# LayerNorm weight and bias moved from the rows into the copies of their transposes

## The chip, the cores and the metric

One core of a Trainium2 chip runs one program. The metric is the device time of one launch in microseconds (us), median over runs. The engines are TensorE (PE for its matmuls, PEld for its weight loads), VectorE (DVE), ScalarE (ACT), GpSimd (POOL) and SyncE (SP), which here only issues DMAs. Each has its own instruction stream; they meet only at semaphores.

## The reference

Two layers over 256 tokens of 1024 channels, all in float32. Each layer is a mixer and then a mixture of experts, and each of these four stages ends in a LayerNorm over the channels. Mixer 0 is an mLSTM beside an RG-LRU, mixer 1 an S5 state space model beside gated linear attention. The experts are 64, of which each token takes 8, plus a shared one. What matters here:

```
def layer_norm(x, w, b):
    xc = x - mean(x)
    y = xc * rsqrt(mean(xc * xc) + EPS)
    return y * w + b

for l in (0, 1):
    h = layer_norm(ALPHA * h + mixer_l(h) @ w_out[l], ln1_w[l], ln1_b[l])
    h = layer_norm(ALPHA * h + moe_l(h),              ln2_w[l], ln2_b[l])
```

ALPHA is the square root of 2. The output is the last h.

## The kernel before, in words

The stages mix0, moe0, mix1, moe1 follow one another on every engine; each engine walks through its own list of them. The 256 tokens are two tiles of 128 rows (t = 0 and 1, one token for each partition), held in `h` of 128 x 2 x 1024. Every stage first needs the transposed rows `hT`, 1024 channels in 8 chunks of 128 partitions by 256 tokens. PE transposes `h` chunk by chunk into four banks of PSUM (L653 in the mixers, L910 before the experts); ACT copies banks 0 and 2 to `hT`, DVE banks 1 and 3 (L1110 and L1326 in mixer 1, L1238 and L1751 before the experts). A copy takes one bank, two chunks, 128x512.

A stage ends in `dve_ln`. For each tile: the sum with the scaled residual (L1307, after the mixers only; after the experts PE has already added it in PSUM), statistics of both halves (L1310), their aggregation (L1312). Then DVE subtracts the mean and multiplies by the weight row `lnw`, half by half (L1316), while ACT takes the root of the variance (`act_ln`, L1281). DVE inverts it (L1320) and forms h, scaled by it, plus the bias row `lnb` (L1321). That signals `h_ready`. Weight and bias stand as rows, copied to every partition by DMA (`sp_ln_params`), and are overwritten for the next stage when `h_ready` says so.

`wait_h` makes the reader of a stage wait for `h_ready`. PE waits so before the transposes of each tile. In between it runs filler matmuls that compute nothing (`keep_clock`, L608): 8 before tile 0 in mixer 1, 5 before tile 1 in front of the experts. SP waits for the same signal before it loads the remaining first experts or the next mixer weights. In mixer 1 PE also runs 64 small matmuls (L640) between the tiles, whose result ACT copies in four parts (L1182) after its copies of the transposed rows. PE's next matmuls (L772) wait for all of these.

Before the experts PE computes router scores from `hT` (L925), and the shared expert's first product (L945) runs while DVE chooses the experts: L1684 adds the router's bias, a chain of small operations follows, and L1720 writes `chosen`. PE needs `chosen` at L951, in the middle of L945. Meanwhile ACT casts h to the upper part `h_top` (L1241, per tile) and GpSimd forms the rest `h_low` (L560, per tile). The router's sigmoid on ACT needs a table load before it. The expert loop then gathers rows from `h_top` and `h_low`, multiplies them with the experts' weights (L1040, L1070) and adds the results in PSUM (L971); its weights stream in by DMA.

The last stage's h goes out by DMA. At the start SP loads x, then a few parameters (L317), then the first mixer's weights (L265), which PE needs for L615.

## Time and profile before

| | |
|---|---|
| runs | 1323.25, 1323.59, 1326.84 us; median 1323.59 |
| profiled execution | 1326.38 us, span 1324.7 us, mean granted clock 0.985 |
| busy in the span | PE 1287.8 (97%), PEld 699.5, DVE 527.7 (40%), ACT 187.4 (14%), POOL 46.7 (4%) |
| chain that ended last | PE 92%, DVE 4%, DMA 3%, issue 1%, ACT 1% |
| the costliest lines of the chain | L1040 33%, L1070 17%, L971 10%, L992 9% |
| DMA | 462.33 MB, mean 349 GB/s |

The three inner boundaries lie near 152 us (mix0 to moe0), 661 us (moe0 to mix1) and 800 us (mix1 to moe1); the last norm begins near 1312 us.

How to read the rows below: a timeline row has the start, the busy time, the engine, the line of the kernel, the operation, what it writes and reads, how many instructions are merged into it, and in brackets how long the engine had been idle and what ended that. A float32 matmul or transpose is recorded as two instructions, so five filler matmuls are x10. A merged row's time runs from the first start to the last end. A table load (ACT_TABLE_LOAD) is ACT's change to the set of functions that its next operation needs.

### The profile page before, as it was taken

How to read it: one execution, taken by the hardware profiler on the slowest of the kernel's cores; microseconds unless marked ns; L12 is line 12 of the kernel's file. 1: busy time of each engine (PE TensorE's matmuls, PEld its weight loads, DVE VectorE, ACT ScalarE, POOL GpSimd, SP SyncE). 2: the span in 40 equal slices, each digit the busy share in tenths (PEclk: the TensorE clock that was granted, in tenths of full speed). 3: DMA queues.
4: the chain of work that ended last, by engine and by line, in shares of the span. 5: the costliest groups of instructions: out<-in, count | busy, mean ns of one | idle time of the engine just before them, and what ended most of it. 6: DMA issues, size and time to landing. Idle time of an engine off the chain costs nothing.

```text
span 1324.7 us, 16993 instructions
## 1 busy us (share of the span) xinstructions
PE 1287.8 (97%) x6753; PEld 699.5 (53%) x6753; DVE 527.7 (40%) x1071; ACT 187.4 (14%) x314; POOL 46.7 (4%) x76
## 2 busy tenths in 40 slices
PE   8979999999999999999999999999999999999996
PEld 6845564445544454445476656454445544454443
DVE  6777543333333333333336136233333333333324
ACT  3122201111111111111031212011111111111111
POOL 6200100000000000000010001000000000000000
PEclk9989999999999999999998998999999999999999
DMA  7853849999999999999952169499999999999992
GB/s 236 245 229 145 350 200 408 421 422 422 422 422 421 423 422 422 422 422 421 376 184 83 33 252 421 166 402 420 421 422 423 422 422 422 422 423 422 421 421 113
DMA packets 77625, 462.33 MB, mean 349 GB/s; under 512 B 9680, under 2 KB 10896, under 8 KB 27152
## 3 DMA queue, kind: packets, MB, share of 16 engines
q1 hardware_dynamic: 77584, 461.74, 86.0%
q8 instruction: 30, 0.49, 0.1%
q14 instruction: 11, 0.09, 0.0%
HBM read 455.36 MB, written 6.36 MB: 349 GB/s over the span
## 4 chain that ended last, share of the span: by engine, by line
PE 92%; DVE 4%; DMA 3%; issue 1%; ACT 1%; SPq 0%; DVEq 0%; ACTq 0%
PE bank L1040 33%; PE bank L1070 17%; PE bank L971 10%; PE bank L992 9%; PE bank L615 4%; PE bank L625 4%; PE bank L945 2%; PE bank L673 2%; PE bank L687 2%; PE bank L1051 1%; DMA expert_weights<-s_rows 1%; PE bank L1004 1%; DVE expert_weights L1531 1%; PE bank L980 1%; DMA weight_ring<-in_w_in_even 1%; PE bank L795 1%
## 5 line engine op out<-in xcount | busy, mean ns | idle before, releaser
L1070 PE MATMUL bank<-expert_weights,hiddenT 128*64 128x512 f32 x1024 | 233.8, 598 | 2.0 <-DVE hiddenT L1807 2.0
L1040 PE MATMUL bank<-expert_weights,hT 128*64 128x512 f32 x1024 | 225.3, 592 | 0.0
L1040 PE MATMUL bank<-expert_weights,weight_ring 128*64 128x512 f32 x1024 | 225.2, 592 | 0.0
L1804 DVE TENSOR_TENSOR hidden<-silu_gate,bank 128x256 f32<-128x256 f32 x64 | 26.9, 421 | 330.0 <-ACT silu_gate L1262 330.0
L1040 PEld LDWEIGHTS bank<-expert_weights,weight_ring 128*64 128x64 f32 x1024 | 74.5, 137 | 145.2 <-issue 145.2
L1040 PEld LDWEIGHTS bank<-expert_weights,hT 128*64 128x64 f32 x1024 | 73.4, 137 | 145.3 <-issue 145.0
L1070 PEld LDWEIGHTS bank<-expert_weights,hiddenT 128*64 128x64 f32 x1024 | 68.2, 136 | 119.7 <-issue 110.7
L992 PE MATMUL bank<-onehot_r,h_top 128*128 128x256 f32 x512 | 125.5, 288 | 0.0
L992 PE MATMUL bank<-onehot_r,h_low 128*128 128x256 f32 x512 | 119.7, 277 | 0.0
L971 PE MATMUL bank<-y_top,onehotT_r 128*128 128x512 f32 x264 | 111.8, 423 | 0.0
L971 PE MATMUL bank<-y_low,onehotT_r 128*128 128x512 f32 x264 | 104.5, 396 | 0.0
L992 PEld LDWEIGHTS bank<-onehot_r,h_low 128*128 128x128 f32 x512 | 96.4, 188 | 0.0
L992 PEld LDWEIGHTS bank<-onehot_r,h_top 128*128 128x128 f32 x512 | 96.3, 188 | 0.0
L615 PE MATMUL bank<-hT,weight_ring 128*128 128x256 f32 x384 | 86.5, 388 | 0.4 <-DMA weight_ring<-in_w_in_even 0.4
L971 PEld LDWEIGHTS bank<-y_top,onehotT_r 128*128 128x128 f32 x264 | 49.4, 187 | 61.8 <-issue 52.4
L1262 ACT ACTIVATE silu_gate<-bank 128x256 f32<-128x256 f32 x64 | 24.5, 383 | 397.9 <-PE bank L1040 397.9
L1266 ACT ACTIVATE y_top<-bank,slot_gate 128x512 fp32r<-128x512 f32 x64 | 44.0, 687 | 259.5 <-PE bank L1070 259.5
L615 PEld LDWEIGHTS bank<-hT,weight_ring 128*128 128x128 f32 x384 | 74.4, 195 | 11.9 <-DMA weight_ring<-in_w_in_even 0.9
L1814 DVE TENSOR_SCALAR y_top<-bank,slot_gate 128x512 fp32r<-128x512 f32 x64 | 48.0, 751 | 78.4 <-PE bank L1070 78.4
L1821 DVE SCALAR_TENSOR_TENSOR y_low<-bank,slot_gate,y_top 128x512 fp32r<-128x512 f32 x64 | 48.0, 751 | 57.5 <-ACT y_top L1266 57.5
L625 PE MATMUL bank<-weight_ring,hT 128*128 128x512 f32 x128 | 58.3, 612 | 8.6 <-DVE gate_cols L1385 8.6
L1807 DVE COPY hiddenT<-bank 128x256 f32<-128x256 f32 x64 | 27.1, 424 | 92.3 <-PE bank L1051 92.3
(359 smaller groups left out, 1073.6 us busy)
## 6 DMA issues: line engine op xcount, KB each, us to landing
expert_weights<-in_exp_w_gate SPq DMA_DIRECT2D x128, 1024.0 KB, 11.1
expert_weights<-in_exp_w_up SPq DMA_DIRECT2D x128, 1024.0 KB, 13.9
expert_weights<-in_exp_w_down SPq DMA_DIRECT2D x128, 1024.0 KB, 13.2
weight_ring<-in_w_in_even SPq DMA_DIRECT2D x6, 2048.0 KB, 10.3
weight_ring<-in_w_out SPq DMA_DIRECT2D x4, 2048.0 KB, 7.4
weight_ring<-in_w_in_odd SPq DMA_DIRECT2D x4, 2048.0 KB, 10.1
s_c<-expert_weights SPq DMA_DIRECT2D x1, 3072.0 KB, 8.7
expert_weights<-s_c SPq DMA_DIRECT2D x1, 3072.0 KB, 10.9
```

The lines of the kernel that those rows point to most:

```text
L615: last = nc.tensor.matmul(B.tile(f"{name}{i}")[:, a * SEQ:(a + 1) * SEQ], w[:, c, (2 * i + a) * P:(2 * i + a + 1) * P], hT[:, c, :], start ...
L625: last = nc.tensor.matmul(B.tile(f"{name}{t}")[:, :], hT[:, c, t * P:(t + 1) * P], w[:, c, :], start=(c == 0), stop=(c == KC - 1))
L673: last = nc.tensor.matmul(bank[2 * t + n][:, :], mixT[:, m0 + m, t * P:(t + 1) * P], w[:, m, n * 512:(n + 1) * 512], start=(m == 0), stop= ...
L971: last = nc.tensor.matmul(bank[2 * t + n][:, :], onehotT[:, par, t, :], part[:, n * 512:(n + 1) * 512], start=False, stop=(done and part i ...
L992: last = nc.tensor.matmul(bank[banks[k // 2]][:, (k % 2) * SEQ:(k % 2 + 1) * SEQ], part[:, t, c, :], onehot[:, t, :, :].rearrange("p a s - ...
L1040: last_mm = nc.tensor.matmul(bank[6][a * CAP:(a + 1) * CAP, :].rearrange("p (w f) -> p w f", w=2), xq[:, c, s0:s0 + CAP], ew_gu(2 * u + a, c),
L1070: last_mm = nc.tensor.matmul(bank[b][a * CAP:(a + 1) * CAP, :], hm[:, j, a * CAP:(a + 1) * CAP], ew_d(2 * u + a)[:, j, half * 512:(half + ...
L1266: nc.scalar.activation(y_top[:, 512:1024], bank[5][:, :], ACT.Copy, scale=slot_gate[:, u:u + 1])\
L1804: nc.vector.tensor_tensor(hslot[:, :], sg[:, :], bank[6][:, DE:2 * DE], ALU.mult)\
L1807: nc.vector.tensor_copy(hm[:, :, :], bank[7][:, 0:JE * P].rearrange("p (j s) -> p j s", j=JE))\
L1814: nc.vector.tensor_scalar(y_top[:, 0:512], bank[4][:, :], slot_gate[:, u:u + 1], None, ALU.mult)\
L1821: nc.vector.scalar_tensor_tensor(out=y_low[:, 512:1024], in0=bank[5][:, :], scalar=slot_gate[:, u:u + 1], in1=y_top[:, 512:1024], op0=ALU. ...
```

## The change

Weight and bias are no longer applied to the rows that get transposed. After the norm of the first three stages DVE forms only x_hat, mean taken off and multiplied by the inverse deviation, in `resid`, and signals `x_hat`. PE transposes x_hat, and `wait_h` waits for that signal, as SP does. In the transposed rows a channel is a partition, so weight and bias are columns (`lncols`, a new 128x48 load at the start), and the copies to `hT` apply them: ACT with `Identity`, scale and bias, DVE with a multiply and an add, each chunk of 128x256 by itself, so two instructions where one copy was. The rows of h are made later (`dve_h`, two operations of 128x1024 for each tile): before the experts, tile 0 inside the norm and tile 1 behind the turned copies; in mixer 1 both behind the copies. ACT's cast to `h_top` now waits for `h_ready`. The last norm (`dve_ln_out`) keeps the product with the weight row, but behind root and reciprocal. `act_ln` starts with a root of a constant, one column, so that the table is asked for before the statistics arrive. Filler goes from 8 matmuls to 2 in mixer 1 and from 5 to 3 before the experts. `wts` now shares the buffer of `masked`, and the mixers share two semaphores.

```diff
         def pe_transposes(pe, B, st):
             for t in range(TT):
                 if stage_no[st] and t == 0:
-                    keep_clock(pe, 7, 8)
+                    keep_clock(pe, 7, 2)
...
-                                                   h[:, t, :].rearrange("p (q c) -> p c q", c=KC)[:, c, :],
-                                                   ident[:, :])
+                                                   (resid if stage_no[st] else h)[:, t, :]
+                                                   .rearrange("p (q c) -> p c q", c=KC)[:, c, :], ident[:, :])
...
                 if t:
-                    keep_clock(pe, 0, 5)
+                    keep_clock(pe, 0, 3)
...
         def act_moe(act, l, chain):
...
-                nc.scalar.copy(hT[:, 2 * b:2 * b + 2, :], bank[4 + b][:, :].rearrange("p (c t) -> p c t", c=2))\
-                  .then_inc(m["hT_a"], 1)
-            for t in range(TT):
+                for c in range(2):
+                    last = act_turned_rows(2 * l, 2 * b + c, bank[4 + b][:, c * SEQ:(c + 1) * SEQ])
+                last.then_inc(m["hT_a"], 1)
+            for t in range(TT):
+                act.wait_ge(S["h_ready"], TT * 2 * l + t + 1)
                 nc.scalar.copy(h_top[:, t, :, :], ...).then_inc(m["top_parts"], 1)
...
         def act_ln(act, k):
             act.wait_ge(S["consts"], N_CONSTS)
+            nc.scalar.activation(spare1[:, 0:1], epsc[:, 0:1], ACT.Sqrt)
...
+        def act_turned_rows(k, c, src):
+            return nc.scalar.activation(hT[:, c, :], src, ACT.Identity, bias=lncols[:, k, 1, c:c + 1],
+                                        scale=lncols[:, k, 0, c:c + 1])
...
+        def dve_ln_stats(dve, chain, k, t, src, summed):
+            for n in range(2):
+                dve.wait_ge(summed, 2 * t + n + 1)
+                if k % 2 == 0:
+                    chain.link(nc.vector.scalar_tensor_tensor(out=src[n], in0=h[:, t, n * 512:(n + 1) * 512],
+                                                              scalar=ALPHA, in1=bank[2 * t + n][:, :],
+                                                              op0=ALU.mult, op1=ALU.add))
+                last = nc.vector.bn_stats(stats[:, t, n, :], src[n])
+            chain.link(last)
+            nc.vector.bn_aggr(mv[:, t, :], stats[:, t, :, :]).then_inc(S["ln_stats"], 1)
+            dve.wait_ge(S["ln_std"], TT * k + t + 1)
+            chain.link(nc.vector.reciprocal(rstd[:, t:t + 1], rstd[:, t:t + 1]))
+
         def dve_ln(dve, chain, k, summed):
             for t in range(TT):
                 src = [bank[2 * t + n][:, :] if k % 2 else resid[:, t, n * 512:(n + 1) * 512] for n in range(2)]
+                dve_ln_stats(dve, chain, k, t, src, summed)
                 for n in range(2):
+                    last = nc.vector.tensor_scalar(resid[:, t, n * 512:(n + 1) * 512], src[n], mv[:, t, 0:1],
+                                                   rstd[:, t:t + 1], ALU.subtract, ALU.mult)
+                last.then_inc(S["x_hat"], 1)
+                if k % 2 == 0 and t == 0:
+                    dve_h(dve, chain, k, t)
+
+        def dve_h(dve, chain, k, t):
+            dve.wait_ge(S["x_hat"], TT * k + t + 1)
+            dve.wait_ge(LN[k]["params"], 32)
+            chain.link(nc.vector.tensor_tensor(h[:, t, :], resid[:, t, :], lnw[:, :], ALU.mult))
+            nc.vector.tensor_tensor(h[:, t, :], h[:, t, :], lnb[:, :], ALU.add).then_inc(S["h_ready"], 1)
+
+        def dve_ln_out(dve, chain, k, summed):
+            for t in range(TT):
+                src = [bank[2 * t + n][:, :] for n in range(2)]
+                dve_ln_stats(dve, chain, k, t, src, summed)
+                dve.wait_ge(LN[k]["params"], 32)
+                for n in range(2):
+                    last = nc.vector.scalar_tensor_tensor(out=resid[:, t, n * 512:(n + 1) * 512], in0=src[n],
+                                                          scalar=mv[:, t, 0:1], in1=lnw[:, n * 512:(n + 1) * 512],
+                                                          op0=ALU.subtract, op1=ALU.mult)
                 chain.link(last)
...
                 nc.vector.scalar_tensor_tensor(out=h[:, t, :], in0=resid[:, t, :], scalar=rstd[:, t:t + 1],
                                                in1=lnb[:, :], op0=ALU.mult, op1=ALU.add).then_inc(S["h_ready"], 1)
+
+        def dve_turned_rows(k, c, src):
+            return nc.vector.tensor_scalar(hT[:, c, :], src, lncols[:, k, 0, c:c + 1], lncols[:, k, 1, c:c + 1],
+                                           ALU.mult, ALU.add)
...
         def dve_mix1(dve, chain):
-            wait_h(dve, "mix1")
             for row in (1, 3):
-                dve_copies(dve, B, f"T{row}", hT[:, 2 * row:2 * row + 2, :])
+                dve.wait_ge(*B.full(f"T{row}"))
+                for c in range(2):
+                    last = dve_turned_rows(1, 2 * row + c, B.tile(f"T{row}")[:, c * SEQ:(c + 1) * SEQ])
+                last.then_inc(B.done["d"], 1)
+            for t in range(TT):
+                dve_h(dve, chain, 1, t)
...
         def dve_moe(dve, l, chain):
...
-                nc.vector.tensor_copy(hT[:, 2 * b:2 * b + 2, :], bank[4 + b][:, :].rearrange("p (c t) -> p c t", c=2))\
-                  .then_inc(m["hT_d"], 1)
+                for c in range(2):
+                    last = dve_turned_rows(2 * l, 2 * b + c, bank[4 + b][:, c * SEQ:(c + 1) * SEQ])
+                last.then_inc(m["hT_d"], 1)
+            dve_h(dve, chain, 2 * l, 1)
             dve.wait_ge(m["halves"], 1)
```

## Rows read from the trace of the kernel before

**Rows 1.** Timeline, first boundary: start us, us, engine line op out<-in, [idle <-releaser].

```profile
152.22 0.69 DVE L1307 SCALAR_TENSOR_TENSOR resid<-h,bank 128x512 f32<-128x512 f32 x1 [1.04 <-PE bank L687]
...
152.90 2.32 PE L608 MATMUL bank<-hT,ident 128*128 128x256 f32 x10
...
153.68 0.21 DVE L1312 BATCH_NORM_AGGREGATE ln_mean_var<-ln_stats 128x2 f32<-128x12 f32 x1
...
153.92 0.29 ACT L1281 ACTIVATE ln_rstd<-ln_mean_var,eps 128x1 f32<-128x1 f32 x1 [6.51 <-DVE ln_mean_var L1312]
...
156.79 1.16 PE L910 MATMUL bank<-ident,h 128*128 128x128 f32 x8 [1.56 <-DVE h L1321]
...
157.54 1.29 DVE L1751 COPY hT<-bank 128x512 f32<-128x512 f32 x2 [0.81 <-PE bank L910]
...
158.27 4.07 ACT L1241 CAST h_top<-h 128x1024 fp32r<-128x1024 f32 x2
...
160.43 5.68 POOL L560 TENSOR_TENSOR h_low<-h,h_top 128x1024 fp32r<-128x1024 f32 x2 [120.03 <-ACT h_top L1241]
...
171.01 0.29 DVE L1720 TENSOR_TENSOR chosen<-replaced,masked 128x128 f32<-128x128 f32 x1
...
171.73 0.33 PE L951 MATMUL bank<-chosen,upper_strict 128*128 128x64 f32 x2
```

**Rows 2.** Timeline of the second boundary, moe0 to mix1.

```profile
663.14 1.28 ACT L1281 ACT_TABLE_LOAD   x1 [3.31 <-DVE ln_mean_var L1312]
...
664.43 3.62 PE L608 MATMUL bank<-hT,ident 128*128 128x256 f32 x16
...
664.44 0.29 ACT L1281 ACTIVATE ln_rstd<-ln_mean_var,eps 128x1 f32<-128x1 f32 x1
...
666.17 1.29 DVE L1310 BATCH_NORM_STATS2 ln_stats<-bank 128x6 f32<-128x512 f32 x2
...
667.49 0.21 DVE L1312 BATCH_NORM_AGGREGATE ln_mean_var<-ln_stats 128x2 f32<-128x12 f32 x1
...
668.87 1.53 PE L640 MATMUL bank<-expert_weights,gathered_xT 128*32 128x96 f32 x64
...
670.59 1.16 PE L653 MATMUL bank<-ident,h 128*128 128x128 f32 x8 [0.19 <-DVE h L1321]
...
672.07 1.91 ACT L1182 COPY expert_weights<-bank 32x384 f32<-32x384 f32 x4
...
674.19 1.07 PE L772 MATMUL bank<-hT,w_gates 128*32 128x256 f32 x16 [2.45 <-ACT expert_weights L1182]
```

**Rows 3.** Windows, first boundary then third: busy us (count) by engine, clock, DMA.

```profile
158.93:162.81 3.88, 3.88 (x26) 3.08 (x27) 1.61 (x3) 3.86 (x3) 2.38 (x1) 1.00 1.00 414
...
807.07:813.86 6.79, 6.79 (x26) 4.54 (x27) 2.52 (x4) 4.67 (x3) 5.24 (x2) 0.55 1.02 425
```

**Rows 4.** Groups by form: count, busy us, mean ns, idle before.

```profile
L1531 DVE TENSOR_TENSOR expert_weights<-expert_weights 128x1024 f32<-128x1024 f32 x6 | 7.2, 1222 | 8.5 <-DMA expert_weights<-s_rows 8.4
...
L1568 DVE TENSOR_SCALAR expert_weights<-bank,cols_odd 128x256 f32<-128x256 f32 x2 | 0.9, 479 | 16.8 <-PE bank L781 16.8
...
L1550 DVE TENSOR_SCALAR expert_weights<-expert_weights 128x512 f32<-128x512 f32 x1 | 0.4, 426 | 0.0
...
L1222 ACT ACTIVATE expert_weights<-bank,cols_odd 128x256 f32<-128x256 f32 x4 | 1.7, 470 | 4.2 <-PE bank L868 4.2
```

**Rows 5.** Chain of waits at the end: start us, us, engine line.

```profile
1318.55 0.22 DVE ln_mean_var L1312
...
1318.80 1.41 DVE resid L1316 x2
```

**Rows 6.** Line L1684: count, ns min/median/max, first and last start us.

```profile
L1684 DVE TENSOR_TENSOR biased<-scores,router_bias x2: 292/1295/2298, 164.0 to 814.6; 128x128 f32<-128x128 f32 x2
```

**Rows 7.** Timeline of the start.

```profile
2.89 0.65 SPq L317 DMA_DIRECT2D cols_even<-in_cols_even  x1
...
16.88 14.08 PE L615 MATMUL bank<-hT,weight_ring 128*128 128x256 f32 x64 [0.41 <-DMA weight_ring<-in_w_in_even]
```

More of the change, by code:

```diff
@@ L383, in sp_moe @@
             if k:
-                sp.wait_ge(S["h_ready"], TT * k)
+                sp.wait_ge(S["x_hat"], TT * k)
             for s in range(early, NSLOT):
@@ L1175, in act_mix1 @@
             B = B1
-            act_copies(act, B, "T0", hT[:, 0:2, :])
-            act_copies(act, B, "T2", hT[:, 4:6, :])
+            for row in (0, 2):
+                act.wait_ge(*B.full(f"T{row}"))
+                for c in range(2):
+                    last = act_turned_rows(1, 2 * row + c, B.tile(f"T{row}")[:, c * SEQ:(c + 1) * SEQ])
+                last.then_inc(B.done["a"], 1)
             act.wait_ge(M1["direct"], 1)
@@ L1299, in dve_ln @@
         def dve_ln(dve, chain, k, summed):
-            ln = LN[k]
             for t in range(TT):
                 src = [bank[2 * t + n][:, :] if k % 2 else resid[:, t, n * 512:(n + 1) * 512] for n in range(2)]
+                dve_ln_stats(dve, chain, k, t, src, summed)
                 for n in range(2):
-                    dve.wait_ge(summed, 2 * t + n + 1)
-                    if k % 2 == 0:
-                        chain.link(nc.vector.scalar_tensor_tensor(out=src[n], in0=h[:, t, n * 512:(n + 1) * 512],
-                                                                  scalar=ALPHA, in1=bank[2 * t + n][:, :],
-                                                                  op0=ALU.mult, op1=ALU.add))
-                    last = nc.vector.bn_stats(stats[:, t, n, :], src[n])
-                chain.link(last)
-                nc.vector.bn_aggr(mv[:, t, :], stats[:, t, :, :]).then_inc(S["ln_stats"], 1)
-                dve.wait_ge(S["ln_stats"], TT * k + t + 1)
-                dve.wait_ge(ln["params"], 32)
-                for n in range(2):
-                    nc.vector.scalar_tensor_tensor(out=resid[:, t, n * 512:(n + 1) * 512], in0=src[n],
-                                                   scalar=mv[:, t, 0:1], in1=lnw[:, n * 512:(n + 1) * 512],
-                                                   op0=ALU.subtract, op1=ALU.mult)
-                dve.wait_ge(S["ln_std"], TT * k + t + 1)
-                chain.link(nc.vector.reciprocal(rstd[:, t:t + 1], rstd[:, t:t + 1]))
@@ L1663, in dve_head_norm @@
                 last = nc.vector.tensor_tensor(hmv[:, :, :, 1], hmv[:, :, :, 1], hrs[:, :, :], ALU.add)
-            last.then_inc(M["hstat"], 1)
-            dve.wait_ge(M["hstd"], 1)
+            last.then_inc(M0["hstat"], 1)
+            dve.wait_ge(M0["hstd"], 1 if center else 2)
             chain.link(nc.vector.reciprocal(hrs[:, :, :], hrs[:, :, :]))
@@ L1857, in _ @@
                     dve_moe(dve, int(st[-1]), chain)
-                dve_ln(dve, chain, stage_no[st], {"mix0": M0["out_full"], "mix1": M1["out_full"],
+                (dve_ln if stage_no[st] < len(stages) - 1 else dve_ln_out)(dve, chain, stage_no[st], {"mix0": M0["out_full"], "mix1": M1["out_full"],
                                                   "moe0": MO[0]["acc_full"], "moe1": MO[1]["acc_full"]}[st])
@@ L1904, in packed, with by_chunk @@
     bt = b.reshape(P, 2, 4, 4, 32).transpose(2, 4, 1, 3, 0)
-    return {"cols_even": even, "cols_odd": odd, "b_odd": b.reshape(P, -1), "c_odd": c.reshape(P, -1),
+    def by_chunk(name, l):
+        return np.asarray(inputs[name])[l].reshape(P, KC)
+    ln = np.stack([np.stack([by_chunk(f"ln{n}_{w}", l) for w in "wb"], axis=1) for n, l in ((1, 0), (2, 0), (1, 1))], axis=1)
+    return {"ln_cols": np.ascontiguousarray(ln.reshape(P, -1), dtype=np.float32), "cols_even": even, "cols_odd": odd, "b_odd": b.reshape(P, -1), "c_odd": c.reshape(P, -1),
             "bt_odd": bt.reshape(P, -1)}
```

26 lines of the change are left out of this document (15 added, 11 removed).

## The prediction

> **What bounds the kernel now.** I read the page first, its busy shares and its chain of waits: PE is busy for 97% of the span and makes up 92% of the chain. Then the list of what PE waited for, to find the few places where it stands still: they add up to under 30 us, and about 10 us of them lie at the three inner boundaries between stages, where a layer norm on DVE and ACT is all that PE can wait for. Last the timeline of each boundary. In the first (mixer 0 to experts 0) PE ends its projection at 152.20; DVE works off the last half tile, and PE transposes the second tile only at 156.79, though the filler matmuls L608 ran out at 155.22 [rows 1]. It stands still again until the copies of the turned rows (L1238, L1751) are done, and goes on at 158.93. The second boundary has the same shape, with a table load on ACT that starts only when the statistics are there, and PE goes on at 674.19 [rows 2]. The third repeats the first to a few hundredths of a microsecond up to L925. After each boundary PE runs without a gap that matters, so what is won or lost there reaches the end; DMA is late nowhere in the expert loops.
>
> The third boundary shows one thing more. From 807.07 to 813.86 the granted clock averages 0.55, nearly all of it at half, the lower level (1.2 GHz). The same 26 records, L925 and the first eight of L945, take 6.79 us there and 3.88 us at the first boundary [rows 3]: a fall of the clock costs 2.91 us. PE had stood still 1.55 us, worked 1.16, stood still 0.98. The first boundary, with the same gaps, kept the clock.
>
> **The base of the sum.** The profiled execution took 1326.38 us (span 1324.7 and 1.7 around it). The runs are 1323.25, 1323.59 and 1326.84. Profile less 2.91 is 1323.47, so I read the median as an execution without a fall, and two of the four executions as having had one.
>
> **The change, part by part.** Tile 0 and tile 1 are the two halves of 128 tokens.
>
> *First boundary, the norm.* After the aggregation DVE now waits for ACT's root (0.03 to start, 0.29, 0.02), does the reciprocal (about 0.2 with its wait), then two subtract-and-multiply of 128x512 from SBUF. Such an instruction with one column takes 0.43 us [rows 4]; the pair of two-tensor ones that it replaces takes 1.41 [rows 5]. Two columns can't be under one: the pair lies between 0.85 and 1.41, I take 1.0. From the aggregation's end (153.89) to the transposes this makes 0.35 + 0.2 + 1.0 + 0.04 = 1.6 where 2.90 stood. But tile 0 now also makes its h inside the norm: root and reciprocal 0.55, the pair 1.0, two tensor operations of 128x1024 at 1.22 [rows 4] with their wait 2.5, together 4.05 against 2.8 (the 2.90 above, less the start of PE). DVE had 1.04 us of room before tile 1's last half [rows 1]; it comes 1.2 later, so 0.2 late. Gain 1.1 (0.7 to 1.4): transposes at 155.7.
>
> *The turned copies.* Two copies of 128x512 on DVE (1.29) become four of 128x256 with two columns. With one column two take 0.88, so about 0.40 apart [rows 4]; four are 1.7 to 1.95, I take 1.8: 0.5 more (0.35 to 0.7). ACT's four at 470 ns each, some 0.37 apart [rows 4], end before them. PE starts L925 0.6 earlier than before.
>
> *Routing.* The h of tile 1 (2.45 us) now stands behind the copies on DVE, 158.3 to 160.8. ACT's cast of tile 1 waits for it: 160.8 to 162.8, then the table load 1.28 and the scores at 164.4, against 163.9. GpSimd's h_low moves too, 5.68 us of work from about 160.8 to 166.5. The row that matters is L1684: 128x128, 2.30 us at the first boundary (from 164.0), ending 0.2 after h_low [rows 1]; at the third, with h_low over before, the same takes 0.29 [rows 6]. So DVE stood behind GpSimd for 2 us. After the change it is released at about 166.6, 0.35 later than now, and with it L1720. Chosen was ready at 171.30 and PE asked at 171.73 [rows 1]; PE comes 0.6 earlier and chosen 0.35 later, so PE waits about 0.35. Net gain 0.25 at this boundary (-0.4 to 0.6), and the same at the third.
>
> *Second boundary.* The root's table is asked for ahead, in an idle stretch of ACT, so 1.28 us leave tile 0. Tile 0: from the aggregation 0.35 + 0.2, then a pair that reads PSUM, where I take 1.45 (1.41 is the pair of the same width now); x_hat at 665.1, where h came when L1310 of tile 1 could start, about 666.2 [rows 2]. Tile 1's statistics follow at once, 1.3 and 0.25 with the aggregation; then 0.55 + 1.45: transposes at 668.6, not 670.59 [rows 2], 2.0 earlier. Filler is 2 matmuls, not 8 (3.62 us, [rows 2]), and ends about when x_hat comes. ACT then reaches L1182 1.48 after the transposes start now (672.07 less 670.59 [rows 2]) and 0.5 later with four copies for two, about 2.0; the 1.91 of L1182, which PE waits for, follow as now. PE goes on at 672.7 to 672.8, gain 1.4 (0.9 to 1.9). The four tensor operations of h (4.9 us) lie under L615, with 14 us to spare before DVE's next reader. SP's loads wait for x_hat and start earlier; its LN parameters wait for h, with nothing urgent behind them.
>
> *The end.* The last norm keeps its form, but the two products now stand behind root and reciprocal, 0.35 + 0.2, where 1.41 of them ran beside the root and only 0.08 of reciprocal showed [rows 5]. For tile 1 that costs 0.5. In tile 0 the saved table load pays for it. Loss 0.55.
>
> *The start.* One more load stands before the first weights on SP; its like (cols_even) took 0.65 us to issue [rows 7]. PE waits for these weights, 0.41 us at 16.88 [rows 7], and the chain of mixer 0 hangs on it. The DMA engines are already full there, so between 0 and 0.65, I take 0.5. Everything else (semaphores, the shared buffer for weights, one more tiny root in the mixer norms, under ACT's idle time) costs nothing.
>
> Sum at full clock: +0.5 - 0.25 - 1.4 - 0.25 + 0.55 = -0.85, so 1322.6.
>
> *The clock.* PE's idle time grows although its work starts sooner. At the second boundary it now stands still 2.44 us [rows 2]; afterwards about 0.65 (from 667.9, when the filler, tile 0's transposes and the 1.53 of L640 are through [rows 2], to 668.6), 1.16 of transposes, then 3.1. At the first and third: 1.35 and 1.55 instead of 1.56 and 0.98, with three filler matmuls for five. The clock fell once in half of the executions with shorter gaps than these. I therefore expect one fall in the typical execution, most likely at the second boundary, at the 2.91 us of [rows 3].
>
> At the second boundary the table load starts at 663.14, when the statistics are there, takes 1.28, and the root starts at 664.44 [rows 2]: nothing but the load stands in between. The Trainium skill, "ScalarE: Activation LUTs" (What ACT_TABLE_LOAD costs), gives about 1283 ns for the load and about 1380 ns more for a drain, 2.66 us for a switch. The trace agrees with the load and shows no room for the drain; by the page's switch the gain of that boundary would be some 1.4 larger, an estimate, and the sum 1321.2 at full clock. The row decides.
>
> **The rivals.**
> - *No fall of the clock:* 1322.6. For it: in two of four executions there was none, and the second boundary kept it with 2.44 us of rest.
> - *Two falls or more:* 1322.6 + 5.8 = 1328.4, slower. All three boundaries have longer gaps than before. Against: in no execution shown does the time ask for two.
> - *DVE loses its turn to GpSimd* (the other side): if ACT's cast of tile 0 ends before the second operation of tile 1's h has started, h_low goes first. By my times the cast ends at 159.9 and that operation starts at 159.6, only 0.3 us apart. The operation then waits until 162.85, h comes at 164.1, the cast 166.15, h_low ends at 169.05, L1684 at 169.3, chosen at 174.35, PE having asked at 171.1 to 171.3. That is 2.7 more at two boundaries: 1322.6 + 5.4 = 1328.0. It decides from 0.3 us of delay on DVE. That one of the two shuts the other out is what L1684 shows, 2.30 beside h_low and 0.29 without [rows 6]. The Trainium skill, "SBUF — State Buffer" (Who interferes with whom), has it as a rule: a Vector instruction with two SBUF inputs and a GpSimd one that reads SBUF exclude each other for the whole instruction, whichever starts first; by that rule, the trace agrees.
> - *The table load doesn't move,* or stays behind the wait: 1.3 is lost at the second boundary and 1.3 at the end against the sum, so 1325.2 without a fall.
>
> **How the numbers follow.** One fall 0.45: 1322.6 + 2.9 = 1325.5, its own range 1323.8 to 1327.3 from the bounds above. No fall 0.26. Two falls 0.12, lost turn 0.08, table load 0.04, something not seen 0.05. A difference of 0.3% is 4.0 us, about what can be told from no change. Slower needs 1327.6: most of two falls and lost turn, 0.16. Faster needs 1319.6, beyond the best ends of all terms (about 1321): 0.04. Same 0.80. Range 1321.5 to 1328.5.
>
> **What would show it.** Right: no table load behind the statistics at the second boundary and the end; transposes 1.1 and 2.0 us after a shorter wait than now; L1720 some 0.35 later against the projection's end, with a short wait of PE at L951; half clock in a window behind the second boundary. Wrong: a first operation of h on DVE of 1.2 and a second of over 3 us (the lost turn); full clock behind all three boundaries (then 1322.6); the weights at the start later by more than 0.65.

## The result, and the profile after

| | before | after |
|---|---|---|
| median of the runs beside each other | 1325.19 us (7 runs, 1323.12 to 1326.84) | 1330.94 us (7 runs, 1327.24 to 1332.37) |
| ratio after / before | | 1.0042, 95% interval 1.0027 to 1.0058 |
| profiled execution, its span | 1326.38, 1324.7 us | 1330.94, 1328.5 us |

The change makes the kernel slower by 0.4%. The forecast was 1325.5 with a range up to 1328.5: the time lies outside, on a side that had been given 0.16.

The span grew by 3.8 us. To find where, I took the same few instructions in both traces as marks and subtracted:

| stretch, from mark to mark | before | after | difference |
|---|---|---|---|
| start to tile 0's transposes before experts 0 | 152.02 | 153.59 | +1.57 |
| to the shared expert's down product (L1004, now L1007) | 25.40 | 26.47 | +1.07 |
| experts 0, to the first statistics of their norm | 484.10 | 486.30 | **+2.20** |
| second boundary, to mixer 1's first product (L772, now L775) | 12.67 | 11.67 | -1.00 |
| mixer 1, to tile 0's transposes before experts 1 | 125.98 | 126.24 | +0.26 |
| third boundary, to L1004, now L1007 | 28.31 | 25.25 | -3.06 |
| experts 1, to the first statistics of the last norm | 484.11 | 486.33 | **+2.22** |
| the last norm, to the end | 12.07 | 12.62 | +0.55 |
| sum | | | +3.81 |

The -3.06 at the third boundary is mostly the clock: the profile before had its fall there (2.91 us, [rows 3]), while the profile after has one at the first boundary and one at the second.

The two bold rows are the surprise. The change touches nothing inside the expert loops, no wait in them grew, and both are longer by the same 2.2 us. The groups of instructions by form show one line that is slower, the gather; the line below is one of its neighbours, which is not. First the kernel before (columns as in [rows 4]):

```profile
L992 PE MATMUL bank<-onehot_r,h_top 128*128 128x256 f32 x512 | 125.5, 288 | 0.0
L992 PE MATMUL bank<-onehot_r,h_low 128*128 128x256 f32 x512 | 119.7, 277 | 0.0
L971 PE MATMUL bank<-y_low,onehotT_r 128*128 128x512 f32 x264 | 104.5, 396 | 0.0
```

After:

```profile
L995 PE MATMUL bank<-onehot_r,h_top 128*128 128x256 f32 x512 | 129.5, 291 | 0.0
L995 PE MATMUL bank<-onehot_r,h_low 128*128 128x256 f32 x512 | 124.1, 281 | 0.0
L974 PE MATMUL bank<-y_low,onehotT_r 128*128 128x512 f32 x264 | 104.5, 396 | 0.0
```

A loop has 512 of these matmuls, half with each part, so 2.2 us are 4.3 ns for each. The view of one line in a narrow window shows that it is every matmul and not a few late ones: minimum, median and maximum in ns, of eight with h_top, in the middle of the loop, before:

```profile
L992 PE MATMUL bank<-onehot_r,h_top x8: 276/276/369, 404.8 to 406.5; 128*128 128x256 f32 x8
```

and after:

```profile
L995 PE MATMUL bank<-onehot_r,h_top x8: 277/281/367, 408.5 to 410.2; 128*128 128x256 f32 x8
```

The boundaries did about what was forecast. The first, to be read against [rows 1]:

```profile
155.58 0.29 ACT L1290 ACTIVATE ln_rstd<-ln_mean_var,eps 128x1 f32<-128x1 f32 x1 [6.67 <-DVE ln_mean_var L1323]
155.91 0.16 DVE L1325 RECIPROCAL ln_rstd<-ln_rstd 128x1 f32<-128x1 f32 x1 [0.36 <-ACT ln_rstd L1290]
156.11 1.00 DVE L1333 TENSOR_SCALAR resid<-resid,ln_mean_var,ln_rstd 128x512 f32<-128x512 f32 x2
...
157.16 1.16 PE L913 MATMUL bank<-ident,resid 128*128 128x128 f32 x8 [1.23 <-DVE resid L1333]
...
157.69 1.93 ACT L1295 ACTIVATE hT<-bank,ln_cols 128x256 f32<-128x256 f32 x4 [1.81 <-PE bank L913]
157.92 1.90 DVE L1362 TENSOR_SCALAR hT<-bank,ln_cols 128x256 f32<-128x256 f32 x4 [0.81 <-PE bank L913]
...
159.92 3.60 PE L928 MATMUL bank<-hT,router_w 128*64 128x256 f32 x16 [1.60 <-ACT hT L1295]
160.98 1.23 DVE L1344 TENSOR_TENSOR h<-h,ln_b 128x1024 f32<-128x1024 f32 x1
161.67 6.09 POOL L563 TENSOR_TENSOR h_low<-h,h_top 128x1024 fp32r<-128x1024 f32 x2 [121.44 <-ACT h_top L1249]
...
166.32 1.59 DVE L1729 TENSOR_TENSOR biased<-scores,router_bias 128x128 f32<-128x128 f32 x1
```

The transposes come 3.57 after those of tile 0 (157.16 less 153.59; 4.77 before), the pair L1333 takes the 1.0 that was forecast, and L928 takes 3.60 where it took 1.95: the clock fell, the granted clock averages 0.52 from 159.92 to 163.45. The second boundary, against [rows 2]:

```profile
664.70 1.28 ACT L1287 ACT_TABLE_LOAD   x1
...
665.99 0.20 ACT L1287 ACTIVATE table_load<-eps 128x1 f32<-128x1 f32 x1
...
666.36 1.29 DVE L1321 BATCH_NORM_STATS2 ln_stats<-bank 128x6 f32<-128x512 f32 x2 [0.76 <-PE bank L974]
...
672.00 1.53 DVE L1333 TENSOR_SCALAR resid<-bank,ln_mean_var,ln_rstd 128x512 f32<-128x512 f32 x2
...
673.58 1.16 PE L656 MATMUL bank<-ident,resid 128*128 128x128 f32 x8 [0.92 <-DVE resid L1333]
674.11 1.93 ACT L1295 ACTIVATE hT<-bank,ln_cols 128x256 f32<-128x256 f32 x4 [2.34 <-PE bank L656]
...
675.92 1.90 ACT L1188 COPY expert_weights<-bank 32x384 f32<-32x384 f32 x4
...
678.03 1.16 PE L775 MATMUL bank<-hT,w_gates 128*32 128x256 f32 x16 [3.29 <-ACT expert_weights L1188]
```

The table load is over before the statistics start. And the end, the chain of waits (start, us, what), against [rows 5]: root and reciprocal now stand in front of the products.

```profile
1322.16 0.30 ACT ln_rstd L1290
1322.47 0.02 issue
1322.49 0.17 DVE ln_rstd L1325
1322.67 0.03 issue
1322.69 1.42 DVE resid L1353 x2
```

### The profile page after: what moved, and what is told of

It is laid out like the page before. It is cut to its first block, busy times and chain, and to the rows that moved or that the text cites. A ratio compares the mean times of both kernels' runs of the same rounds, so it can differ in the third digit from the quotient of the medians.

```text
span 1328.5 us, 16971 instructions
## 1 busy us (share of the span) xinstructions
PE 1284.2 (97%) x6733; PEld 697.1 (52%) x6733; DVE 536.8 (40%) x1083; ACT 191.1 (14%) x324; POOL 47.3 (4%) x76
## 4 chain that ended last, share of the span: by engine, by line
PE 90%; DVE 5%; DMA 3%; ACT 1%; issue 1%; SPq 0%; DVEq 0%
PE bank L1043 33%; PE bank L1073 17%; PE bank L974 10%; PE bank L995 9%; PE bank L618 4%; PE bank L628 4%; PE bank L676 2%; PE bank L948 1%; PE bank L1054 1%; DMA expert_weights<-s_rows 1%; PE bank L1007 1%; DVE expert_weights L1572 1%; PE bank L690 1%; PE bank L983 1%; DMA weight_ring<-in_w_in_even 1%
## 5 line engine op out<-in xcount | busy, mean ns | idle before, releaser
L995 PE MATMUL bank<-onehot_r,h_top 128*128 128x256 f32 x512 | 129.5, 291 | 0.0
L995 PE MATMUL bank<-onehot_r,h_low 128*128 128x256 f32 x512 | 124.1, 281 | 0.0
```

The lines of the kernel that those rows point to most:

```text
L995: last = nc.tensor.matmul(bank[banks[k // 2]][:, (k % 2) * SEQ:(k % 2 + 1) * SEQ], part[:, t, c, :], onehot[:, t, :, :].rearrange("p a s - ...
```

## The experiments

**What could lengthen one matmul of the loop?** The change put two new buffers in front of others in SBUF: `ln_cols` (192 bytes per partition) and `table_load` (32 with its rounding). Everything allocated behind them moved. `onehot`, which the gather streams, went from byte 183360 to 183584, that is from 64 to 32 beyond a multiple of 128. Moving the buffers behind all others tests it:

```diff
-        lncols = sb("ln_cols", [P, 3, 2, KC])
...
-        spare1 = sb("table_load", [P, 1])
...
         prm = sb("s5_work", [P, 13, NT])
+        lncols = sb("ln_cols", [P, 3, 2, KC])
+        spare1 = sb("table_load", [P, 1])
```

> The changed kernel with ln_cols and table_load allocated behind all other buffers, so that onehot starts at byte 183360 of a partition again instead of 183584; no instruction differs. Theory A (the gather matmuls L995 are slower because onehot, their moving operand, now starts at 32 beyond a multiple of 64 bytes): 16 of them take 1.83 us again instead of 1.90, each expert loop 473.0 and 484.1 us on the same stretches instead of 475.2 and 486.3, the kernel about 4.4 us faster than the changed one (near 1326.5). Theory B (something in the changed instruction streams, or in what h and h_top hold, slows the loops): the loops stay 2.2 us longer each and the time stays near 1330.9.

Measured: 1325.28 us (12 runs), ratio to the kernel before 0.9993 (0.9979 to 1.0007); expert stages of 483.97 us each.

```profile
L995 PE MATMUL bank<-onehot_r,h_top 128*128 128x256 f32 x512 | 125.2, 287 | 0.0
L995 PE MATMUL bank<-onehot_r,h_low 128*128 128x256 f32 x512 | 119.4, 277 | 0.0
```

So the slowdown of the loops is where the buffers lie, and without it the changed kernel can't be told from the kernel before. Then the same the other way round, the kernel before with 32 unused bytes and no other edit:

```diff
+        pad = sb("pad", [P, 8])
         onehot_at = next_offset()
```

> The kernel before with 32 unused bytes in front of onehot, which then starts at 183392, 32 beyond a multiple of 64; nothing else differs. Theory A: the gather matmuls L992 take 1.90 us for 16, each expert loop 2.2 us longer, the kernel about 4.4 us slower than before (near 1329.6 against 1325.2). Theory B: no difference from before.

Measured: 1329.57 us (10 runs), ratio 1.0038 (1.0023 to 1.0053), expert stages of 486.05 us. Its groups:

```profile
L993 PE MATMUL bank<-onehot_r,h_top 128*128 128x256 f32 x512 | 129.0, 291 | 0.0
L993 PE MATMUL bank<-onehot_r,h_low 128*128 128x256 f32 x512 | 123.5, 280 | 0.0
```

This is 4.36 us above the kernel before (1325.21), as theory A had it. Every buffer behind onehot moves with it in these kernels; that onehot is the one that counts rests on the gather being the only one of the costly groups that loses more than 2 ns (L971 with y_top goes from 423 to 425).

**Which starts are good?** The same edit in the changed kernel (onehot at 64 beyond a multiple of 128), and one of 64 bytes in the kernel before (at 0).

> The changed kernel with 32 more unused bytes in front of onehot: it starts at 183616, a multiple of 64 that neither kernel had. Theory A: gather back at 1.83 us for 16, loops 4.4 us shorter together. If instead the old address itself or the distance to another buffer mattered, it stays at 1.90. Theory B: stays at 1.90.

> The kernel before with 64 unused bytes in front of onehot: start 183424, a multiple of 64 and of 128 (before it was 64 beyond a multiple of 128). Theory A with 64 bytes as the unit: gather at 1.83 us for 16 as before. If a coarser or another boundary counts: another value, shorter or longer than 1.83.

Measured: the first 1325.13 us (one run), expert stages 484.3 and 484.2, 287 and 277 ns: fast. The second 1328.32 us (one run), 486.57 for each, 292 and 281 ns: slow, so a multiple of 64 is not enough. Next I moved everything from the weight ring on by 64, the gather's two stationary parts with it (h_top lies in `resid`, h_low in the ring):

```diff
+        pad = sb("pad", [P, 16])
         wring_at = next_offset()
```

> The kernel before with 64 unused bytes per partition in front of the weight ring, so that the ring (with h_top and h_low in it), h, hT, resid and onehot all start 64 bytes further: onehot at 0 beyond a multiple of 128 as in the slow kernel with 64 bytes in front of onehot alone, but as far from h_top and h_low as in the kernel before. Theory 1, the distance between onehot and h_top/h_low decides: the gather matmuls stay at 288 and 277 ns, 16 of them at 1.83 us, the expert loops at 473.0 and 484.1 us, time about 1325. Theory 2, onehot's own start decides (fast only 64 beyond a multiple of 128): 292 and 281 ns, 1.90 us, loops at 475.3 and 486.3, time about 1329.

Measured: 1324.87 us, 484.0 and 484.1, 287 and 277 ns, with onehot at the same start modulo 128 as in the slow kernel ahead of it. So not onehot's own start decides, but how it stands to other buffers. Which? First h_top and onehot together, h_low left (the same line, in front of `resid_at`):

> The kernel before with 64 unused bytes in front of resid, so that h_top (which lies in resid) and onehot start 64 bytes further and h_low (in the weight ring) stays: the distance from h_top to onehot is again 64 beyond a multiple of 128, that from h_low to onehot is 0. Theory 1a, the distance between onehot and the rows that the same matmul holds decides: the h_top group stays at 287 to 288 ns, the h_low group goes to 280 to 281, each loop 1.1 us longer, time 1327. Theory 1b, the distance between onehot as it streams and the rows that are being loaded for the next matmul decides (half of each part's loads lie under the other part): both groups in between, 290 and 279. Rival, the start of h_top or h_low alone decides: one of 1a's numbers would come with no change in the other kernel whose every start was moved, which stayed at 288 and 277, so then both stay or both change.

Measured: 1329.05 us, 486.3 for each, and both groups slow, where theory 1a had wanted h_top's to stay fast and 1b half of each:

```profile
L993 PE MATMUL bank<-onehot_r,h_top 128*128 128x256 f32 x512 | 129.0, 292 | 0.0
L993 PE MATMUL bank<-onehot_r,h_low 128*128 128x256 f32 x512 | 123.7, 281 | 0.0
```

Neither form held. Three more separate the two parts from each other and from their neighbours: h_top alone moved (64 bytes in front of `resid`, 64 in front of onehot), h_low alone (below), and h_low with onehot (below, with `ln_stats` behind onehot and 32 bytes in its place).

```diff
-        wring = sb("weight_ring", [P, 2, KC * 512])
+        wring = sb("weight_ring", [P, 2, KC * 512 + 16])
...
-            offset=wring_at + 4 * (KC * 512 * (ring_no[f"sh_d{l}"] % 2) + JE * D))
+            offset=wring_at + 4 * ((KC * 512 + 16) * (ring_no[f"sh_d{l}"] % 2) + JE * D) + 64 * (1 - ring_no[f"sh_d{l}"] % 2))
```

> The kernel before with h_top's start 64 bytes further (resid moved), h_low where it was, and onehot 128 bytes further, so still 64 beyond a multiple of 128. Starts modulo 128: h_top 64, h_low 0, hT 0, onehot 64. Theory L, the distance from h_low to onehot must be 64: fast, 287 and 277 ns, expert stages of 484.0 us. Theory B, the distances from both parts must be 64: slow, 292 and 281 ns, 486.3 us. Theory N, it is counted from something else that lies with the weight ring, h or hT: fast, as L.

> The kernel before with 64 unused bytes behind each of the two slots of the weight ring and h_low at 64 beyond a multiple of 128 in its slot; h, hT, h_top and onehot move by 128. Starts modulo 128: h_top 0, h_low 64, hT 0, onehot 64. Theory L: slow, 281 and 292 ns, expert stages of 486.3 us. Theory B: slow too. Theory N: fast, 484.0 us.

> The same with onehot 64 bytes nearer, at a multiple of 128. Starts modulo 128: h_top 0, h_low 64, hT 0, onehot 0. Theory L: fast, 287 and 277 ns, expert stages of 484.0 us, although onehot lies where it was slow. Theory B: slow, 486.3 us. Theory N: slow, 486.3 us.

Measured: 1328.04, 1327.77 and 1330.78 us (one run each). All kernels in one table, starts modulo 128:

| h_top | h_low | onehot | expert stages, us | kernels |
|---|---|---|---|---|
| 0 | 0 | 64 | 484.0 to 484.3 | before; changed with the buffers moved; changed with 32 bytes |
| 64 | 64 | 0 | 484.0 to 484.1 | before, all moved by 64 |
| 0 | 0 | 32 | 486.3 | the change |
| 0 | 0 | 96 | 486.1 | before with 32 bytes |
| 0 | 0 | 0 | 486.6 | before with 64 bytes |
| 64 | 0 | 0 | 486.3 | h_top and onehot moved |
| 64 | 0 | 64 | 485.7 | h_top alone |
| 0 | 64 | 64 | 486.3 | h_low alone |
| 0 | 64 | 0 | 485.5 | h_low and onehot |

Theories L and N fall with the last three rows. What is left is theory B: as fast as before only where onehot starts 64 beyond a multiple of 128 from both parts. Theory B alone doesn't give the sizes, and they differ: where the distance to h_top alone is right (rows six and eight) the cost is all of the 2.3 us, where that to h_low alone is (rows seven and nine) it is 1.5 to 1.7. Nor does it give which group is slow: with h_top alone moved (row seven) h_top's takes 289 ns and h_low's stays at 277, where theory B had 292 and 281; with h_low and onehot moved (row nine) they take 290 and 282. Most rows rest on one profile, but its two expert stages agree within 0.15 us in each. Why 64, and which access meets which, stays open.

**The table load alone.** The kernel before with the early root in `act_ln` and nothing else of the change:

```diff
             act.wait_ge(S["consts"], N_CONSTS)
+            nc.scalar.activation(spare1[:, 0:1], epsc[:, 0:1], ACT.Sqrt)
```

> The kernel before with one thing of the change: ACT asks for the root's table ahead of each norm, by a root of one column of a constant (its output column behind all other buffers, onehot stays). The products that ran beside the load (1.41 us) cover it and the root except for some 0.25 us. Theory: the table load is gone from the second boundary and the end, and each gains 0.25 us: 1324.7. Rival: the load is placed in front of the real root all the same, and nothing changes.

Measured: 1323.72 us (10 runs), ratio 0.9998 (0.9985 to 1.0010): not to be told from no change in the time, but plain in the trace. The end takes 11.71 us where 12.07 stood, the second boundary 12.41 where 12.67 stood. There the load is over 0.38 before the statistics, and root and first product start together:

```profile
660.91 1.28 ACT L1280 ACT_TABLE_LOAD   x1
...
662.20 0.20 ACT L1280 ACTIVATE table_load<-eps 128x1 f32<-128x1 f32 x1
662.57 1.29 DVE L1312 BATCH_NORM_STATS2 ln_stats<-bank 128x6 f32<-128x512 f32 x2 [0.77 <-PE bank L972]
...
664.15 0.29 ACT L1283 ACTIVATE ln_rstd<-ln_mean_var,eps 128x1 f32<-128x1 f32 x1 [1.74 <-DVE ln_mean_var L1314]
664.15 1.41 DVE L1318 SCALAR_TENSOR_TENSOR resid<-bank,ln_mean_var,ln_w 128x512 f32<-128x512 f32 x2
```

**Start and end undone.** From here on the changed kernel has its buffers at the end. The `ln_cols` load goes behind the first two blocks of weights, and `dve_ln_out` gets its old order back, the reciprocal behind the products:

```diff
-                dve_ln_stats(dve, chain, k, t, src, summed)
+                for n in range(2):
+                    dve.wait_ge(summed, 2 * t + n + 1)
+                    last = nc.vector.bn_stats(stats[:, t, n, :], src[n])
+                chain.link(last)
+                nc.vector.bn_aggr(mv[:, t, :], stats[:, t, :, :]).then_inc(S["ln_stats"], 1)
+                dve.wait_ge(S["ln_stats"], TT * k + t + 1)
                 dve.wait_ge(LN[k]["params"], 32)
...
+                dve.wait_ge(S["ln_std"], TT * k + t + 1)
+                chain.link(nc.vector.reciprocal(rstd[:, t:t + 1], rstd[:, t:t + 1]))
```

> The changed kernel with its two new buffers behind all others (so onehot starts where it did before), the ln_cols load behind the first two blocks of weights, and the last norm in the old order (products beside the root). Theory: both losses that were not in the expert loops are undone, 0.8 to 1.0 us at the start and 0.55 at the end less 0.26 for the table load now asked for early; against the version with only the buffers moved (1325.3) it is 1.3 to 1.8 faster: 1323.7, faster than the kernel before by about 1.1 us (0.1%), which five rounds may just tell. Rival: the start is no dearer by that load (the first filler-free matmul of mixer 0 came at 16.4 to 17.1 us in kernels with and without it), then 1324.7 and no difference from before.

Measured: 1323.92 us (12 runs), ratio 0.9987 (0.9971 to 1.0003). The end takes 11.72 us, 0.90 less than after the change. The start can't be told: the first matmul on the weights came at 16.87 us here; it comes at 16.42 to 17.90 in the four profiles with the load in front, and at 16.03 to 17.14 in the other thirteen.

**The filler.** The counts back to 8 and 5:

```diff
-                    keep_clock(pe, 7, 2)
+                    keep_clock(pe, 7, 8)
...
-                    keep_clock(pe, 0, 3)
+                    keep_clock(pe, 0, 5)
```

> The changed kernel with the two new buffers moved to the end and the filler back at 8 and 5 matmuls. At the old counts the filler ends 4.9 us after the statistics of tile 0 at the second boundary and delays tile 1's transposes by less than 0.1 us; before the experts it ends 0.4 us ahead of x_hat. Theory 1, the shortened filler is what lets the clock fall: full clock behind all three boundaries in the profile, a mean 2 to 3 us under that of the version with 2 and 3 (1324.8), so about 1322.3. Theory 2, the falls come with the shape of the boundaries (two short waits with a burst of transposes between) whatever the filler: one or two falls as before, time 1325 within 0.7.

Measured: 1326.52 us (12 runs), ratio 1.0014 (0.9997 to 1.0032). In its one profile theory 1 is half right: behind the second boundary the clock stayed (L775 1.07, its successors 14.08), behind the first it fell all the same. The time forecast from it, 1322.3, did not come. And my price for the filler was wrong: eight matmuls end after x_hat and put the transposes 8.81 after the first statistics (672.09 less 663.28), where two leave them at 7.22. So 1.6 us are paid at each launch for a fall saved, which in mixer 1 costs 0.6 to 2.3 (below).

**Work in the waits instead.** A filler ahead of the transposes delays them. The idle time behind them is longer (3.29 and 1.60), and nothing can be delayed there as long as the filler is shorter than the wait. A new helper multiplies the identity by itself, since `hT` is being written then. The filler ahead of the transposes goes from 2 to 3 and from 3 to 5 in the same edit, so against the last version two things change:

```diff
+        def keep_short(pe, b, count):
+            for _ in range(count):
+                nc.tensor.matmul(bank[b][:, 0:P], ident[:, :], ident[:, :], start=True, stop=True)
...
-                    keep_clock(pe, 7, 2)
+                    keep_clock(pe, 7, 3)
...
+            if stage_no[st]:
+                keep_short(pe, 3, 20)
             for b in range(4):
                 pe.wait_ge(*B.read(f"T{b}"))
...
-                    keep_clock(pe, 0, 3)
+                    keep_clock(pe, 0, 5)
...
+            keep_short(pe, 0, 9)
             pe.wait_ge(m["hT_a"], 2)
```

> The changed kernel as in the last version (buffers moved, ln_cols later, last norm in the old order), with PE kept busy in the waits that followed each burst of transposes: 20 matmuls of 128x128 on the identity (about 145 ns each, 2.9 us) in the 3.29 us ahead of mixer 1's first product, 9 (1.3 us) in the 1.60 us ahead of the router's product, and the filler ahead of tile 1 at 5 and at 3. None of it is longer than the wait that it fills. Theory: half clock behind the second boundary (in every profile with the filler at 2) and behind one of the other two comes from PE standing still there, so it goes: full clock behind all three, about 2.0 us less in mixer 1 and 1.5 to 2.9 at the first or third, 1323.9 less 3.5 to 4.9, 1319.0 to 1320.4: faster than the kernel before by 0.3%. Rival: the clock falls whatever PE does there, 1323.9 with half clock in the same places.

> The kernel before with the same short matmuls in its own waits behind the transposes: 15 (2.2 us) in the 2.45 us ahead of mixer 1's first product, 6 (0.9 us) in the 0.98 us ahead of the router's. Theory: as most profiles of this form show one fall at one of the three boundaries, 1.5 to 2.9 us go: 1324.8 less 2.2, 1322.6, and full clock behind all three. Rival: the wait of 1.55 us ahead of tile 1's transposes, which stays, is what lets the clock fall, then 1324.8 with a fall at the first or third boundary.

Measured: 1323.99 us (12 runs), ratio 0.9992 (0.9981 to 1.0002), and for the kernel before with 15 and 6 of them 1325.55 us (12 runs), 1.0007 (0.9996 to 1.0018). In both profiles the clock stayed full behind all three boundaries, as the theory said. That is not the filler ahead of the transposes alone: with 8 and 5 there and the waits empty the clock fell at the first boundary, and the kernel before had the same 8 and 5. But the time did not come. One part is that 40 records of L616 took 4.63 us, 231 ns for each matmul and not 145, so the filling outlasted the waits. In mixer 1 that costs 1.1 us (the second boundary takes 12.78 for 11.67). Before the experts L936 starts 0.35 late, and it costs nothing: the stretch to the shared expert's down product stays at 25.25, because PE would have waited for `chosen`. The falls saved are 3.25 us against the profile of the last version (26.23 less 25.25 at the first boundary, 127.67 less 125.40 in mixer 1), so 2.1 should have been left. In the profile mixer 0, where nothing was changed, took 2.2 us longer (154.00 for 151.76) and offset them; whether it does so in the median too no run shows. In the kernel before, 15 and 6 outlast the waits as well (13.50 for 12.67 at the second boundary, 25.68 for 25.39 at the others), but mixer 1 is 2.2 shorter (123.79 for 125.97), so its median of 1325.55 stays unexplained. (The 145 ns were a transpose's, eight in 1.16 us. A transpose is one record here, as x8 for eight chunks in [rows 1] shows, and not two as said above; a float32 matmul is two, 28 records for 14.) Cut to 14 and 6:

> The last changed version with its filling cut to the waits: a short matmul takes 231 ns where it was taken for 145, so 20 of them outlasted mixer 1's wait by 1.1 us and 9 the router's by 0.35. Now 14 (3.2 us in 3.29) and 6 (1.45 in 1.60). Theory: full clock behind all three boundaries as with 20 and 9, and the 1.8 us of overrun are back: 1324.0 less 1.8, 1322.2, faster than the kernel before by 0.1 to 0.2%. Rival: without the overrun the clock falls again behind the second boundary, then the overrun's 1.1 us are traded for a fall and the time stays at 1324. In the profiles mixer 0 varies by 3.5 us (its end at 150.5 to 154.0 us) with half clock at 60 to 90 us, so only the mean over runs can tell 2 us, and barely.

Measured: **1320.51 us** (6 runs, 1317.36 to 1321.89), ratio 0.9967 (0.9954 to 0.9980), the one version that beats both kernels. Its timeline, first and second boundary:

```profile
155.15 1.16 PE L920 MATMUL bank<-ident,resid 128*128 128x128 f32 x8 [0.37 <-DVE resid L1341]
156.15 1.50 PE L616 MATMUL bank<-ident 128*128 128x128 f32 x12
157.91 1.95 PE L936 MATMUL bank<-hT,router_w 128*64 128x256 f32 x16 [0.26 <-ACT hT L1303]
...
669.00 3.29 PE L616 MATMUL bank<-ident 128*128 128x128 f32 x28
672.45 1.07 PE L782 MATMUL bank<-hT,w_gates 128*32 128x256 f32 x16 [0.16 <-ACT expert_weights L1196]
```

L936 at 1.95 and L782 at 1.07 are the durations at full clock, against 3.60 and up to 1.93 at half. The waits left, 0.26 and 0.16, show that the filling now fits. From the first statistics to L782 it takes 11.67 us (672.45 less 660.78), as after the change, so nothing is paid for it. Against the profile of the version with empty waits it saves 1.0 at the first boundary and 2.1 in mixer 1, together 3.1, and the medians differ by 3.4 (1323.92 less 1320.51): this the trace explains. Against 20 and 9 matmuls the medians differ by 3.5, and the fit is worth only 1.1 of it (11.67 for 12.78); 2.4 lie in mixer 0 in the two profiles (151.57 for 154.00), and six runs don't settle how much of that is chance.

## Why the prediction was wrong

**The step that failed** is the sentence at the end of the start: "Everything else (semaphores, the shared buffer for weights, ...) costs nothing". The two new buffers are not even in that list. They cost 2.20 and 2.22 us in the expert loops, 4.4 of the 5.4 us between forecast and result. With that undone and all else as changed, the time is 1325.28, and the forecast had been 1325.5. That agreement is luck: two errors cancel, the base and the clock. The forecast was 1.9 us above the median that it started from (1323.59), and measured beside the kernel before, the version with the buffers moved is 0.07 above it, with an interval that ends at 0.9.

- *The base.* I read 1323.59 as an execution without a fall. It was the median of three; the later medians are 1325.19 (7 runs), 1325.21 (23), 1324.45 (29), 1324.49 (23) and 1324.37 (11). The three profiles of this form with a fast gather and empty waits (before, all moved by 64, table alone) have one fall each. So the usual execution seems to hold a fall already, and the base was 0.8 to 1.6 too low.
- *First and third boundary, forecast -0.25 each.* At full clock 25.25 (after, third boundary) against 25.39 to 25.40 (the kernel before with 32 and 64 bytes, first boundary): -0.15. The norm gained the 1.2 that was forecast as 1.1. My net gain of 0.25 was a wrong sum besides: with chosen ready 0.43 before PE asks, 0.35 later and PE 0.6 earlier, PE waits 0.52 and not 0.35, and 0.08 is left.
- *Turned copies, +0.5.* DVE's four took 1.90, inside the 1.7 to 1.95. From transposes to L928 it is 2.76 for 2.14, +0.6. The idle time is put down to ACT, but ACT's four were over at 159.62, DVE's at 159.82, and L928 began at 159.92.
- *Second boundary, -1.4.* Measured -1.00. The transposes came 1.85 earlier (forecast 2.0); ACT reached the next copies 2.34 after the transposes, where 2.0 was forecast and 1.48 stood: its four copies took 1.93, and that term was sized from a form that reads less expensively in [rows 4], 1.7 for four.
- *Routing.* Chosen came late, as forecast: at the third boundary PE waited 0.2 (0.35). L1729 took 1.59.
- *The end, +0.55:* +0.55.
- *The start, +0.5:* not resolved. Mixer 0's end lies between 150.48 and 154.00 us in the 17 profiles, for kernels that differ there in the one load at most, with half clock between 60 and 90 us for different times. The +1.57 of the table is within that. The weights came at 17.90 us in the profile after, 1.02 later than before, which I had named as a sign of being wrong; the three other profiles with the load in front have 16.42 to 16.93, against 16.88 before, so no run shows it to be the load's price.
- *The clock, one fall of 2.91.* The profile after has two, at the first boundary and the second, as the second rival had it, but they cost far less than the row they were sized from. The first: 26.47 against 25.24 without a fall (the changed kernel with 32 bytes), 1.2 us. The second: mixer 1 took 126.24, and 127.67 to 127.69 in three other profiles with a fall, against 125.40 to 125.61 without one (filler at 8, and the two with the waits filled), so 0.6 to 2.3. Whether a part is given back behind it can't be told: PE's gap at L798 is 1.46 to 2.28 us in the four with a fall and 2.06 without. Only at the third boundary does a fall cost the 2.9 of [rows 3] (28.31 and 28.29 against 25.39, two profiles of the kernel before's form). All four profiles with the filler at 2 have the fall behind the second boundary, whatever their gather; of the ten with the filler at 8 and the waits not filled, six have it. That fits the fear about the shorter filler and doesn't show it, since the changed kernel with 8 has only one profile; that the longer gaps do so at the first boundary no run shows.
- *The rivals.* The lost turn did not happen: L1344 took 1.23 and GpSimd started 0.69 after it, where I had put 0.3. The table load moved.

As a sum: -0.15, -1.00, -0.15, +0.55 and the loops' 4.42 make 3.67 at full clock without the start. In the two profiles +1.57 of the start comes on top, falls of 1.2 and 0.6 against one of 2.9, and 0.4 less in mixer 1 without a fall (125.61 for 125.97): the 3.8 of the spans. The medians differ by 5.75, with an interval from 3.6 to 7.7.

## What to carry to other kernels

A new buffer in front of others is an edit to every instruction that reads what lies behind it. After a change that allocates, compare the groups by form for operations that the change does not touch, and allocate new things last. Where a clock fall is to be prevented, put the filler in a wait that nothing can be delayed in, and measure one filler instruction before choosing the count: 20 and 9 matmuls measured like none, 14 and 6 took 0.3%, and of the difference between the two the trace gives a third to the count.

## What the runs showed of the hardware

- A gather matmul of 128x256 went from a median of 276 ns to one of 281 when the start of its moving operand was no longer 64 bytes, modulo 128, from those of both stationary parts: 2.2 us in 512 of them. In the other slow kernels the two groups have medians of 279 to 283, but for h_low's in the kernel with h_top alone moved, which stays at 277. The neighbours that stream `hT` or weights (598, 592 ns) did not change in any of the kernels, those that read y by 3 ns at most (423 to 426, 393 to 396). The Trainium skill, "SBUF — State Buffer" (Operand start alignment), asks for a start at a multiple of the element size and gives no speed with it; all of these starts satisfy that, and the trace shows that they are not equal in time.
- Of the ten profiles with the filler at 8 and the waits not filled, the six with a fall behind the second boundary are just the six whose gather is slow, and the four with 484 us for the stage ahead of it have none there. The boundary itself is the same in nine of them (a wait of 2.44 to 2.48 us ahead of L772, or its number there; 3.29 in the changed kernel with 8). But the slow gather is not shown to be the cause: the same six have no fall at the first boundary either, which lies ahead of any gather, and three of the other four do. So a fall may as well hang on the one before it. What links them was not tried.
- The table load of 1.28 us is followed 0.01 later by the root (664.70 and 665.99), also where the load runs ahead of any need for it.
- Four copies of 128x256 from PSUM with bias and scale as columns take 1.93 us in a row on ACT, 0.48 each, and 1.90 on DVE with two columns.
